# ScalarE's order within an attention step: the copy of a turned block before the next item's exponential

## The chip, the core and the metric

The kernel runs on one core of one Trainium2 chip. The metric is the device time of one execution in microseconds (us), lower is better. Where several runs are given, their median counts. The core's engines each work off a queue of their own in order: TensorE (PE: matrix products and turns, that is transposes), VectorE (DVE), ScalarE (ACT), GpSimd (POOL) and SyncE (SP, which here issues DMAs). They wait for each other on semaphores.

## The reference

Two transformer blocks over 512 tokens of width 1024, in float32. The first has two kinds of attention heads and a convolved, gated feed-forward network (FFN), the second a compressed, a selected/windowed and a sliding-window attention between two FFNs. The edit touches only how the attention phases run. Their mathematics, cut to what matters:

```python
# first block: 4 heads "diff" (two softmax maps, one minus lam times the other)
logits = einsum('bhmqd,bhmkd->bhmqk', q, k) * scale + bias      # masked to k <= q
p = softmax(logits, axis=-1)
out = (p[:, :, 0] - lam * p[:, :, 1]) @ v
# first block: 8 heads "stick breaking"
z = (q @ k.T) * scale
between = cumsum(log_sigmoid(-z), reverse=True) - log_sigmoid(-z)   # over k < q
out = where(strict, exp(log_sigmoid(z) + between), 0) @ v
# second block: 8 heads with keys of the whole past, in two branches, gated and added
out = g[1] * softmax(s_selected) @ v_s + g[2] * softmax(s_window) @ v_w + g[0] * o_compressed
# second block: 8 heads with a window of 128 keys and a sink logit
p = softmax(concat([s, sink]))[..., :-1];  out = p @ v
```

With 512 tokens the selected branch and the wide window both see the whole causal past, so the kernel computes both as dense causal softmax.

## The kernel before

Each product of activations with weights is made as three products of split numbers (a high and a low part of weights and activations), with 128 rows of the contraction and 512 tokens at a time. The weights come in units of 512 KB through a ring of six buffers: SP loads one, ScalarE makes its high part (L531), GpSimd its low part (L543), TensorE uses both.

**The attention phases.** There are two, each run by the same four functions, `pe_attn`, `act_attn`, `dve_attn` and `pool_attn`. The work is a list of *items*. An item is a block of 128 queries of one head (of both maps of one diff head) with its keys, 128 to 512 wide. The first phase has 48 items (kinds `sb`, stick breaking, and `diff`), the second 96 (kind `soft`; the last 32, numbers 64 to 95, have the window of at most 256 keys and a sink). An item m goes through these stations:

1. TensorE, the scores (L930), into PSUM; those of two items m and m+1 (m even) together, for diff items each alone.
2. VectorE prepares the logits in SBUF and their smallest negated value, which is the shift (L1043), or the scan of the stick breaking (L1035 to L1040, after three instructions of ScalarE, L973 to L977).
3. ScalarE, the exponential into the tile `W` (named `sq` in the profile): L984 for sb, L988 twice for diff, L994 for soft, behind one of a single column for the sink, L993. The sum of the row comes with it.
4. VectorE, the reciprocal of the sum (L1067), the gate (L1070) or the sink (L1066), or for diff the combination of both maps (L1056 to L1062).
5. TensorE, the *turn*: up to four transposes of 128x128 (L945) into one of two PSUM banks.
6. ScalarE, the *copy* of the turned block to the tile `WT` (named `tmp` in the profile), L1001.
7. TensorE, the product with V (L954), always into the same PSUM bank.
8. VectorE moves the output out of that bank (L1014, L1017 or L1019).

Every engine runs through steps n. TensorE in step n makes the scores of n and n+1 (n even), then a first part of the fill, the turn of n-2, a second part of the fill, and the product with V of n-3. It waits before the turn for the exponential (diff: the combination) of n-2, and before the product for the copy of n-3 and for the move of output n-4. VectorE in step n moves output n-4, prepares n, and does station 4 for n-1, for which it waits for the exponential of n-1. ScalarE in step n makes its three instructions for an sb item n, the exponential of n-1 and the copy of n-2. Behind that come the *hooks* of the step: a weight unit's high part (L531), the split of queries or keys (L822), the compressed branch's pieces.

**The fill** is what hides all this from TensorE: products of later projections with their weights (L1133, L1122, and L1173 to L1177 for the compressed branch's small network), dealt out by two tables with a number of products for each step. The tables `FILL1` and `FILL2` hold 6 to 8 products a step in most of the first phase and 4 (later 3 to 8) in the second, a pair meaning those before and behind the turn:

```python
FILL2 = [4] * 48 + [6] * 4 + [0] + [6] * 4 + [0] + [3] * 8 + [0] + [3] * 8 + [0] + [3] * 8
FILL2 = FILL2 + [(0, 4), 0] + [(0, 4), (3, 0)] * 5 + [(3, 12), (12, 6), 6]
```

The 16 names of the second fill are used up in order, so a 4 can stand for wide products (512 columns) or for narrow ones (256).

Of the kernel before, what the change touches and what calls it, by code (L numbers as in the profile page):

```python
# [36 lines left out]
ACT = mybir.ActivationFunctionType  # L37
# [164 lines left out]
def build(nc, weights, x_t, params, rows, table_t, bias_line, out_t):  # L202
    with ExitStack() as top:
# [77 lines left out]
        W, WT = sq, tmp  # L281
# [12 lines left out]
        def LM(m, n):  # L294
            return (L0, L1)[m][:, n % 2, :]
# [21 lines left out]
        PS = top.enter_context(nc.psum_tensor("PS", [P, 8, T], F32))  # L317
# [487 lines left out]
        T_PS, PV_PS = 3, 5  # L805
# [154 lines left out]
        def act_attn(act, a, link, after):  # L960
            items = a.items
            for n in range(len(items) + 2):
                for what in a.hooks["act0"].get(n, []):
                    what(act)
                if n < len(items) and items[n].kind == "sb":
                    it = items[n]
                    if n >= 2 and items[n - 2].kind == "diff":
                        act.wait_ge(a.comb, n - 1)
                    elif n >= 2:
                        act.wait_ge(a.s_read, items[n - 2].map0 + 1)  # L970
                    act.wait_ge(a.qk_done, n + 1)
                    z = LM(0, n)[:, 0:it.nk]
                    c = link(act.activation(z, PS[:, it.bank[0], 0:it.nk], ACT.Abs))  # L973
                    after(c)
                    c = link(act.activation(z, z, ACT.Exp, scale=-1.0))
                    after(c)
                    act.activation(z, z, ACT.Ln, bias=1.0).then_inc(a.pre_done, 1)  # L977
                if 1 <= n < len(items) + 1:
                    it = items[n - 1]
                    if it.kind != "diff" and it.n >= 2:  # L980
                        act.wait_ge(a.turned, it.n - 1)
                    act.wait_ge(a.s_read, it.map0 + len(it.maps))
                    if it.kind == "sb":
                        act.activation(W[:, it.n % 2, 0:it.nk], LM(1, it.n)[:, 0:it.nk], ACT.Exp).then_inc(a.exp_done, 1)  # L984
                    elif it.kind == "diff":
                        for m in range(2):
                            z = LM(m, it.n)[:, 0:it.nk]
                            x = act.activation(z, z, ACT.Exp, bias=it.st[:, 2 + m:3 + m], scale=-1.0,  # L988
                                               accum_out=it.st[:, 4 + m:5 + m])
                        x.then_inc(a.exp_done, 1)  # L990
                    else:
                        if it.sink is not None:
                            act.activation(it.st[:, 5:6], it.sink, ACT.Exp, bias=it.st[:, 2:3], scale=-1.0)  # L993
                        act.activation(W[:, it.n % 2, 0:it.nk], LM(0, it.n)[:, 0:it.nk], ACT.Exp,  # L994
                                       bias=it.st[:, 2:3], scale=-1.0, accum_out=it.st[:, 4:5]).then_inc(a.exp_done, 1)
                if n >= 2:
                    it = items[n - 2]
                    act.wait_ge(a.turned, it.n + 1)
                    if it.n >= 2:
                        act.wait_ge(a.pv_done, it.n - 1)  # L1000
                    act.activation(WT[:, it.n % 2, 0:it.nk], PS[:, T_PS + it.n % 2, 0:it.nk], ACT.Copy).then_inc(a.wt_ready, 1)  # L1001
                for what in a.hooks["act"].get(n, []):
                    what(act)

# [665 lines left out]
        def _(act):  # L1670
# [56 lines left out]
            act_next(act, U_DV + 3)  # L1727
            act.preload_act_table_set("natural_log_exp_and_others")
            act_attn(act, at1, link, after)
            act_head(7)(act)  # L1730
            act_turn1(act, 0, 6)
# [50 lines left out]
            act.wait_ge(v_ready[1], TB)  # L1782
            act.activation(gates[:, :, :], V[:, 0, :, 3 * P:NAT2], ACT.Exp, scale=-1.0).then_inc(gate_e, 1)
            act_attn(act, at2, link, after)
            act_turn1(act, 1, 6)
            act_next(act, U_WO2)
# [272 lines left out]
```

## Time and profile before

| | us |
|---|---|
| median of 3 runs | 1677.44 |
| lowest and highest | 1674.91, 1680.5 |
| the profiled execution | 1680.9 |
| its span, first to last instruction | 1678.9 |
| first attention phase in the trace | about 76 to 250 |
| second attention phase | about 1058 to 1274 |

In that execution TensorE is busy for 98% of the span, VectorE and ScalarE for 42% each, GpSimd for 46%. The times in the trace are from the span's start. A row of a timeline has start, duration, engine, line, operation, and what it writes and reads; in brackets, how long the engine had been idle and what ended that. Instructions of TensorE overlap, and so, by some hundredths, do those of ScalarE.

### The profile page before, as it was taken

Reading aid. Unit: us, or ns where it says so; the run is one execution under the profiler, and the core shown is the slowest. Engines: PE = TensorE matmul, PEld = TensorE weight load, DVE = VectorE, ACT = ScalarE, POOL = GpSimd, SP = SyncE. Lnnn points to the kernel's source line nnn. Section 1 sums busy time; section 2 is a strip of 40 time slices with the busy share of each in tenths; the row PEclk is TensorE's granted clock in tenths of the full one; section 3 lists DMA queues with packets and bytes.
Section 4 is the critical chain, followed back from the end, with each engine's and each line's share of the span. In section 5 each row is a group of like instructions: output and inputs, shape, how many; then the busy total and the mean of one; then the engine's idle time right before and its main releaser. Section 6 shows DMA issues by size and latency. Waiting matters only on the chain.

```text
span 1678.9 us, 21453 instructions
## 1 busy us (share of the span) xinstructions
PE 1645.6 (98%) x8168; PEld 1357.1 (81%) x8168; DVE 706.5 (42%) x1402; ACT 697.7 (42%) x1231; POOL 780.4 (46%) x594
## 2 busy tenths in 40 slices
PE   9999989999999999999999999999999999999997
PEld 7777778888888887888888888888778888888885
DVE  6266654884444226312212225655673311112224
ACT  6367755543334224422223225566573422223322
POOL 7434525474445552744444553644112554444550
PEclk9999989999999999999999999999999999999999
DMA  5411102322322331322322322222002322332231
GB/s 200 145 51 51 39 14 100 101 89 100 101 94 94 101 100 51 120 94 100 100 90 99 101 94 94 89 71 70 26 27 76 100 91 98 101 98 91 100 101 50
DMA packets 42117, 147.37 MB, mean 88 GB/s; under 512 B 4768, under 2 KB 5152, under 8 KB 42016
## 3 DMA queue, kind: packets, MB, share of 16 engines
q1 hardware_dynamic: 40536, 143.13, 25.9%
q10 hardware_dynamic: 1480, 2.89, 0.5%
q8 instruction: 65, 1.06, 0.3%
q14 instruction: 36, 0.29, 0.1%
HBM read 142.84 MB, written 3.41 MB: 87 GB/s over the span
## 4 chain that ended last, share of the span: by engine, by line
PE 88%; DVE 5%; ACT 2%; issue 2%; POOL 1%; DMA 1%; DVEq 0%; ACTq 0%; POOLq 0%
PE PS L499 20%; PE PS L501 20%; PE PS L500 20%; PE PS L1133 5%; PE PS L1122 4%; PE PS L954 4%; PE PS L930 3%; PE PS L474 3%; PE PS L945 2%; PE PS L481 1%; PE PS L521 1%; POOL w_lo L543 1%; PE PS L523 1%; PE PS L522 1%; DMA stage<-in_weights 1%
## 5 line engine op out<-in xcount | busy, mean ns | idle before, releaser
L543 POOL TENSOR_TENSOR w_lo<-stage,w_hi 128x512 fp32r<-128x512 f32 x524 | 710.9, 1382 | 703.5 <-ACT w_hi L531 702.9
L531 ACT ACTIVATE w_hi<-stage 128x1024 fp32r<-128x1024 f32 x262 | 274.6, 1056 | 514.0 <-DMA stage<-in_weights 513.8
L499 PE MATMUL PS<-H_hi,w_hi 128*128 128x512 f32 x992 | 387.7, 391 | 0.4 <-DVE rcol L1311 0.4
L501 PE MATMUL PS<-H_hi,w_lo 128*128 128x512 f32 x992 | 386.0, 389 | 0.0
L500 PE MATMUL PS<-H_lo,w_hi 128*128 128x512 f32 x992 | 386.0, 389 | 0.0
L499 PEld LDWEIGHTS PS<-H_hi,w_hi 128*128 128x128 f32 x992 | 186.2, 188 | 39.7 <-issue 1.0
L500 PEld LDWEIGHTS PS<-H_lo,w_hi 128*128 128x128 f32 x992 | 186.2, 188 | 39.6 <-issue 1.0
L501 PEld LDWEIGHTS PS<-H_hi,w_lo 128*128 128x128 f32 x992 | 186.2, 188 | 39.0
L499 PE MATMUL PS<-A_hi,w_hi 128*128 128x512 f32 x528 | 205.7, 390 | 0.4 <-DVE A_lo L653 0.4
L501 PE MATMUL PS<-A_hi,w_lo 128*128 128x512 f32 x528 | 205.5, 389 | 0.0
L500 PE MATMUL PS<-A_lo,w_hi 128*128 128x512 f32 x528 | 205.4, 389 | 0.0
L668 DVE TENSOR_TENSOR conv<-PS,rstd 128x512 f32<-128x512 f32 x88 | 56.5, 685 | 353.2 <-PE PS L501 337.1
L653 DVE TENSOR_TENSOR A_lo<-A,A_hi 128x512 fp32r<-128x512 f32 x66 | 84.0, 1279 | 227.2 <-ACT A_hi L597 227.2
L499 PEld LDWEIGHTS PS<-A_hi,w_hi 128*128 128x128 f32 x528 | 99.1, 188 | 21.8 <-DVE A_lo L653 1.3
L500 PEld LDWEIGHTS PS<-A_lo,w_hi 128*128 128x128 f32 x528 | 99.1, 188 | 20.7
L501 PEld LDWEIGHTS PS<-A_hi,w_lo 128*128 128x128 f32 x528 | 99.1, 188 | 20.4
L954 PEld LDWEIGHTS PS<-V,tmp 128*128 128x128 f32 x672 | 94.9, 195 | 22.1 <-issue 10.1
L954 PE MATMUL PS<-V,tmp 128*128 128x64 f32 (+1 forms) x672 | 95.4, 271 | 8.2 <-DVE O L1017 3.1
L1001 ACT ACTIVATE tmp<-PS 128x256 f32<-128x256 f32 (+3 forms) x144 | 59.4, 413 | 91.9 <-PE PS L945 91.0
L678 DVE SCALAR_TENSOR_TENSOR conv<-tmp,par,conv 128x511 f32<-128x511 f32 (+1 forms) x88 | 77.4, 934 | 6.2 <-ACT conv L620 5.8
L1133 PE MATMUL PS<-H_hi,w_hi 128*128 128x512 f32 x168 | 74.7, 445 | 0.0
L1133 PE MATMUL PS<-H_hi,w_lo 128*128 128x512 f32 x168 | 71.5, 426 | 0.0
(241 smaller groups left out, 2187.8 us busy)
## 6 DMA issues: line engine op xcount, KB each, us to landing
stage<-in_weights SPq DMA_DIRECT2D x262, 512.0 KB, 3.3
out_t<-Y SPq DMA_DIRECT2D x8, 256.0 KB, 2.0
X<-in_x_t SPq DMA_DIRECT2D x3, 512.0 KB, 8.2
bias_line<-bias_line ACTq DMA_DIRECT2D x1, 1270.0 KB
strip<-bias_line ACTq DMA_DIRECT2D x1, 1024.0 KB, 5.0
stage<-in_weights SPq DMA_DIRECT2D x2, 256.0 KB, 4.4
X<-in_x_t ACTq DMA_DIRECT2D x2, 256.0 KB, 5.8
V<-QF SPq DMA_DIRECT2D x4, 128.0 KB, 2.6
```

Source lines behind the costliest of these rows:

```text
L499: pe.matmul(out, a, h_hi, start=first, stop=False, skip_group_check=skip)
L500: pe.matmul(out, a, h_lo, start=False, stop=False, skip_group_check=skip)
L501: return pe.matmul(out, b, h_hi, start=False, stop=last, skip_group_check=skip)
L531: act.activation(w_hi[:, slot, :], stage[:, slot, :], ACT.Copy).then_inc(hi_done, 1)
L543: lo = pool.tensor_tensor(w_lo[:, slot, cols], stage[:, slot, cols], w_hi[:, slot, cols].bitcast(F32), ALU.subtract)
L653: dve.tensor_tensor(A_lo[:, f % DEEP, :], A[:, f, :], A_hi[:, f % DEEP, :].bitcast(F32), ALU.subtract).then_inc(a_lo_done, 1)
L668: dve.tensor_tensor(z[j], PS[:, pair_bank(n) + j, :], rstd[:, :], ALU.mult).then_inc(zs, 1)
L678: dve.scalar_tensor_tensor(out=y, in0=z[j][:, 0:T - back], scalar=c, in1=y, op0=ALU.mult, op1=ALU.add).then_inc(conv_step, 1)
L954: mm = pe.matmul(PS[:, PV_PS, 0:it.dv], WT[:, it.n % 2, bass.ts(kb, P)], it.v[kb], start=(kb == 0), stop=(kb == it.nk // P - 1))
L1001: act.activation(WT[:, it.n % 2, 0:it.nk], PS[:, T_PS + it.n % 2, 0:it.nk], ACT.Copy).then_inc(a.wt_ready, 1)
L1122: mm = pe.matmul(PS[:, j, :], w[:, u % RING, cols], h, start=(g == 0 and x == 0), stop=(g == 7 and x == 2))
L1133: mm = pe.matmul(PS[:, bank, :], w[:, u % RING, bass.ts(k, P)], h[:, k, :], start=(k == 0 and x == 0), stop=(k == KC - 1 and x == 2))
```

## The change

In `act_attn` the piece with the copy (station 6, for item n-2) moves up, ahead of the piece with the exponential (station 3, for item n-1). The three sb instructions of item n stay first and the hooks last. Nothing else is changed. Line numbers move by it: the copy is L983 in the changed kernel, the exponentials are L990 (sb), L994 (diff), L999 (sink) and L1000 (soft).

```diff
                     act.activation(z, z, ACT.Ln, bias=1.0).then_inc(a.pre_done, 1)
+                if n >= 2:
+                    it = items[n - 2]
+                    act.wait_ge(a.turned, it.n + 1)
+                    if it.n >= 2:
+                        act.wait_ge(a.pv_done, it.n - 1)
+                    act.activation(WT[:, it.n % 2, 0:it.nk], PS[:, T_PS + it.n % 2, 0:it.nk], ACT.Copy).then_inc(a.wt_ready, 1)
                 if 1 <= n < len(items) + 1:
                     it = items[n - 1]
...
                         act.activation(W[:, it.n % 2, 0:it.nk], LM(0, it.n)[:, 0:it.nk], ACT.Exp,
                                        bias=it.st[:, 2:3], scale=-1.0, accum_out=it.st[:, 4:5]).then_inc(a.exp_done, 1)
-                if n >= 2:
-                    it = items[n - 2]
-                    act.wait_ge(a.turned, it.n + 1)
-                    if it.n >= 2:
-                        act.wait_ge(a.pv_done, it.n - 1)
-                    act.activation(WT[:, it.n % 2, 0:it.nk], PS[:, T_PS + it.n % 2, 0:it.nk], ACT.Copy).then_inc(a.wt_ready, 1)
```

ScalarE's queue in the second phase, from the exponential of item 39 to the copy of item 40, before. `tmp<-PS` is the copy, `sq,stat<-L,stat` the exponential, and the brackets name the semaphores waited for (`turned`: the turn is done; `s_read`: VectorE has prepared the item):

```order
L994 ACTIVATE sq,stat<-L,stat 128x256 [waits at2_s_read,at2_turned]
L1001 ACTIVATE tmp<-PS 128x256 [waits at2_pv_done,at2_turned]
L531 ACTIVATE w_hi<-stage 128x1024 [waits loaded5]
L994 ACTIVATE sq,stat<-L,stat 128x384 [waits at2_s_read,at2_turned]
L1001 ACTIVATE tmp<-PS 128x256 [waits at2_pv_done,at2_turned]
L994 ACTIVATE sq,stat<-L,stat 128x384 [waits at2_s_read,at2_turned]
L1001 ACTIVATE tmp<-PS 128x384 [waits at2_pv_done,at2_turned]
```

The same place after:

```order
L983 ACTIVATE tmp<-PS 128x256 [waits at2_pv_done,at2_turned]
L1000 ACTIVATE sq,stat<-L,stat 128x256 [waits at2_s_read,at2_turned]
L531 ACTIVATE w_hi<-stage 128x1024 [waits loaded5]
L983 ACTIVATE tmp<-PS 128x256 [waits at2_pv_done,at2_turned]
L1000 ACTIVATE sq,stat<-L,stat 128x384 [waits at2_s_read,at2_turned]
L983 ACTIVATE tmp<-PS 128x384 [waits at2_pv_done,at2_turned]
L1000 ACTIVATE sq,stat<-L,stat 128x384 [waits at2_s_read,at2_turned]
```

Each copy has moved ahead of the exponential that stood before it; the hook (`w_hi<-stage`) keeps its place. The first phase, where the fourth diff item of the first group (512 keys) meets the next group's first sb item, before:

```order
L977 ACTIVATE L<-L 128x128 [waits act_self]
L988 ACTIVATE L,stat<-L,stat 128x512 [waits at1_s_read]
L988 ACTIVATE L,stat<-L,stat 128x512
L1001 ACTIVATE tmp<-PS 128x384 [waits at1_pv_done,at1_turned]
L973 ACTIVATE L<-PS 128x128 [waits at1_qk_done,at1_comb]
```

And after:

```order
L977 ACTIVATE L<-L 128x128 [waits act_self]
L983 ACTIVATE tmp<-PS 128x384 [waits at1_pv_done,at1_turned]
L994 ACTIVATE L,stat<-L,stat 128x512 [waits at1_s_read]
L994 ACTIVATE L,stat<-L,stat 128x512
L973 ACTIVATE L<-PS 128x128 [waits at1_qk_done,at1_comb]
```

Here both exponentials of the diff item now stand behind the copy, and so behind the turn that it waits for. The instructions of TensorE, VectorE, GpSimd and SP keep their order.

## Rows read from the trace of the kernel before

**Rows 1.** The page, busy us, share of the span and instructions

```profile
PE 1645.6 (98%) x8168; PEld 1357.1 (81%) x8168; DVE 706.5 (42%) x1402; ACT 697.7 (42%) x1231; POOL 780.4 (46%) x594
```

**Rows 2.** Busy time by stretch (stretch, its us; each engine's busy us; granted clock, DMA)

```profile
76.00:240.00 164.00, 154.85 (x962) 124.32 (x961) 113.94 (x283) 114.85 (x283) 69.09 (x57) 0.97 0.13 43
1058.00:1274.00 216.00, 209.04 (x1527) 174.78 (x1526) 125.16 (x533) 131.71 (x377) 68.25 (x51) 0.98 0.16 50
```

**Rows 3.** Waits of TensorE and its weight loads: total us, times, longest

```profile
PE PS L954 <- ACT tmp L1001: 1.0, 3, 0.5
...
PEld PS L954 <- ACT tmp L1001: 4.9, 6, 1.5
```

**Rows 4.** Waits of ScalarE

```profile
ACT tmp L1001 <- PE PS L945: 91.0, 74, 5.9
...
ACT L L973 <- PE PS L936: 15.8, 15, 1.7
```

**Rows 5.** Timeline, items 24 and 25: turns, copy 24, exponential 25, product 24

```profile
1109.10 0.49 PE L945 MATMUL PS<-ident,sq 128*128 128x128 f32 x3
...
1109.62 0.49 ACT L1001 ACTIVATE tmp<-PS 128x384 f32<-128x384 f32 x1 [0.33 <-PE PS L945]
...
1110.01 0.61 ACT L994 ACTIVATE sq<-L,stat 128x384 f32<-128x384 f32 x1
...
1110.29 0.49 PE L945 MATMUL PS<-ident,sq 128*128 128x128 f32 x3
1110.52 0.19 ACT L994 ACTIVATION_READ_ACCUMULATOR sq<-L,stat 128x1 f32 x1
...
1110.85 0.78 PE L954 MATMUL PS<-V,tmp 128*128 128x64 f32 x6
```

**Rows 6.** Timeline: end of exponential 37, copy 36, VectorE's move 35, product 36

```profile
1135.26 0.19 ACT L994 ACTIVATION_READ_ACCUMULATOR sq<-L,stat 128x1 f32 x1
...
1135.35 0.37 ACT L1001 ACTIVATE tmp<-PS 128x256 f32<-128x256 f32 x1
...
1136.11 0.28 DVE L1014 SCALAR_TENSOR_TENSOR O<-PS,stat,O 128x64 f32<-128x64 f32 x1 [0.21 <-DVE stat L1070]
...
1136.54 0.52 PE L954 MATMUL PS<-V,tmp 128*128 128x64 f32 x3 [0.25 <-ACT tmp L1001]
```

**Rows 7.** Timeline, items 68 and 69 of the window part

```profile
1218.95 0.38 PE L945 MATMUL PS<-ident,sq 128*128 128x128 f32 x2
...
1219.37 0.38 ACT L1001 ACTIVATE tmp<-PS 128x256 f32<-128x256 f32 x1 [1.73 <-PE PS L945]
...
1219.65 0.28 ACT L993 ACTIVATE stat<-row,stat 128x1 f32<-128x1 f32 x1
...
1220.23 0.19 ACT L994 ACTIVATION_READ_ACCUMULATOR sq<-L,stat 128x1 f32 x1
1220.31 0.38 PE L945 MATMUL PS<-ident,sq 128*128 128x128 f32 x2
...
1220.76 0.55 PE L954 MATMUL PS<-V,tmp 128*128 128x64 f32 x4
```

**Rows 8.** Timeline, diff items 10 and 11 of the first phase

```profile
115.96 0.49 PE L945 MATMUL PS<-ident,sq 128*128 128x128 f32 x3
116.00 0.71 ACT L988 ACTIVATE L<-L,stat 128x512 f32<-128x512 f32 x1
...
117.32 0.19 ACT L988 ACTIVATION_READ_ACCUMULATOR L<-L,stat 128x1 f32 x1
...
117.41 0.47 ACT L1001 ACTIVATE tmp<-PS 128x384 f32<-128x384 f32 x1
...
118.86 0.66 PE L945 MATMUL PS<-ident,sq 128*128 128x128 f32 x4 [0.34 <-DVE sq L1062]
```

**Rows 9.** Busy time by stretch, TensorE's granted clock in the third column from the right

```profile
1192.00:1200.00 8.00, 5.25 (x36) 4.12 (x36) 6.74 (x24) 3.78 (x8) 0.00 (x0) 1.00 0.01 2
1200.00:1208.00 8.00, 8.00 (x40) 6.86 (x41) 3.32 (x15) 2.46 (x7) 0.00 (x0) 0.57 0.00 1
```

## The prediction, made before the changed kernel had run

> **What bounds the kernel now.** I read the page's busy times first, then the busy times by stretch, the waits of TensorE and of ScalarE, and last the timeline of single steps. TensorE is busy for 98% of the span [rows 1], and it stays at 94% and 97% in the two attention phases, the only places that the edit touches [rows 2]. So a ScalarE instruction costs or gives time only where TensorE stands still for it. The weight products that fill the attention steps are the cover: TensorE has other work while a block goes through ScalarE and VectorE. The cover differs from step to step. The score products of two items are issued together, in the even steps; in an odd step of the second phase there lie only the fill, one turn and one product with V between two turns. I call those the short steps. ScalarE is not short of time: it waits 91.0 us in 74 places for a turn to end before it copies the block [rows 4].
>
> **What the change does to the order.** Let m be an item. Before, ScalarE makes exp(m) as soon as VectorE has prepared it, and then waits for turn(m-1) to copy that block. So exp(m) is usually finished while TensorE is still on its way to turn(m-1). After, ScalarE waits for turn(m-1), copies, and only then makes exp(m). No instruction is added or taken; 142 pairs change places, DMAs and the queues of SP and GpSimd keep theirs. The wait that becomes new is exp(m) behind turn(m-1), and behind exp(m) stand turn(m) on TensorE and, on VectorE, the sum's reciprocal, the gate and the move of output m-2 out of the one PV bank, for which product m-1 waits.
>
> **First term, the leg to the next turn.** An item of the second phase, 384 keys wide: turn(24) ends at 1109.10 + 0.49 = 1109.59, the copy takes 0.49 and starts 0.03 later, exp(25) with its sum takes from 1110.01 to 1110.52 + 0.19, that is 0.70 [rows 5]. ACT's instructions overlap by 0.06. In the new order exp(25) ends at 1109.62 + 0.49 - 0.06 + 0.70 = 1110.75 and turn(25) can start 0.05 later, at 1110.80. It started at 1110.29 [rows 5]: 0.5 us late. In the window part an item has a sink exponential too: turn(68) ends 1219.33, copy 0.38, exponentials 1219.65 to 1220.42 (0.77), new end 1220.46, turn(69) 0.2 us late [rows 7]. In the even steps the score products lie between, and the same sum leaves 0.5 to 2 us of margin.
>
> **Second term, the leg through VectorE.** The trace of before shows this leg where exp was not ahead: exp(37) ends 1135.26 + 0.19 = 1135.45, reciprocal and the gate's multiply follow, the output is moved from 1136.11 to 1136.39, and product 36 starts at 1136.54 [rows 6]. That is 1.09 us from the end of the exponential to the product with V; with the small differences between items I take 1.0. In the new order that ends at 1110.75 + 1.0 = 1111.75 for product 24, which started at 1110.85 [rows 5]: 0.9 late. For product 68 it is 1220.46 + 1.0 = 1221.46 against 1220.76 [rows 7]: 0.7. The later of the two legs is the stall of the step, the first one is contained in it. The same rows say what the wait list's ScalarE entries are worth: the trace puts 0.25 us of product 36 on the copy [rows 6], but the copy of that item ended at 1135.35 + 0.37 = 1135.72 [rows 6], and the product came 0.15 us after VectorE's move. So the 1.0 us in 3 places that TensorE seems to wait for copies (4.9 us on its weight loads) [rows 3] are this leg already, and I count no gain from the earlier copy.
>
> **The sum.** I worked both legs for each item, carrying the delay along (turns, products, moves and hooks later by all stalls so far). Second phase: items 1 to 16 stall 6 times, 1.1 us together (the fill there is four 512-column products, the cover just holds); items 17 to 48, 14 times, 8.6 us (no or narrower fill beside the short steps; [rows 5] is one of them); items 49 to 64, 4 times, 1.5 us; items 65 to 80, 8 times, 5.7 us ([rows 7] is one); items 81 to 95, 13 times, 4.7 us. That is 21.6 us. Between 1184 and 1200 us VectorE also has the compressed branch's work between the reciprocal and the move; where exp comes late there it holds that up too, by under 1 us at two steps, which I leave to the range. First phase: a stick-breaking item's exponential is one instruction of 0.3 to 0.6 us and in the even steps ScalarE waits for the score products anyway (15.8 us in 15 places) [rows 4], so I count 0.1. A diff item's is two of 0.71 with their sums, 116.00 to 117.51, and VectorE needs 1.35 us to combine them before the turn at 118.86. New: turn(10) ends 116.45, copy 0.47, exponentials end 118.40, turn(11) can start 1.35 later at 119.75, 0.9 late [rows 8]. Per group of four diff items that gives 1.05, 1.05, 1.3 and, in the last group whose short step has no fill, 1.7: with the 0.1 it is 5.2. All of it lies on the path, because TensorE has nothing else in its queue order. **Sum: 21.6 + 5.2 = 26.8 us.** The profiled execution took 1680.9 us (span 1678.9), 3.5 over the median of the three runs; on its own base that is 1707.7, on the median 1677.4 + 26.8 = 1704.2. I take **1704**.
>
> **Rivals.** *Only the first leg.* If VectorE's moves have slack that I miss, the stalls are those of the turns: 8.6 in the second phase and 5.2 in the first, 13.8 us, 1691. Against it is that [rows 6] shows the leg acting; for it that I add delays item by item, which may count one twice.
> *The clock.* Behind a stretch in which TensorE was busy for 5.25 of 8 us its mean granted clock over the next 8 us was 0.57 [rows 9]: the lower of its two levels (1.2 GHz) for most of them, which cost 8 x 0.43 = 3.4 us. Stalls of 0.7 to 0.9 us in every 3.5 us would leave TensorE busy for some 78%, between that stretch (66%) and the mean of the phase (97% at a mean clock of 0.98) [rows 2]. One to four more such stretches cost 3 to 13 us: 1707 to 1717, taken as 1713. The Trainium skill (TensorE: Matmul & The Clock Gate, "A second HAM failure mode: psum-queue depth-cycling") says that frequent short idles between groups of matmuls can make the clock go back and forth. By that rule the dips would come all along both phases, against which only the rows of before speak, where short idles kept the clock.
> *Faster: copies free TensorE.* If the waits listed on the copy are real, the earlier copy removes them, 1.0 + 4.9 us [rows 3], and 1677.4 - 5.9 = 1671.5. It decides this way if the copy, not the move, releases the product with V, and if the exponentials' delay of 1 to 3 us stays within the cover, that is if TensorE's distance from one turn's end to the next turn's start is over 1.2 us (copy, exponential and two hand-overs). In [rows 5] it is 0.70. The Trainium skill (PSUM — Partial Sum Buffer, "Summary: rules for kernel authors") advises to evacuate promptly, which is what the edit does; by that rule it would come out on this side.
> *No change.* The delays fall into idle time that is there already (TensorE is idle for 7.0 us in the second phase [rows 2]); 1677 to 1682. Against it: that idle lies at other steps.
> That the edit doesn't take effect is excluded by the instruction order, which shows the exchange at every step.
>
> **How the numbers follow.** Both legs as worked, 1695 to 1713: 0.62, likeliest. First leg only: 0.12. Clock on top: 0.13. No change: 0.06. Faster: 0.07. A measurement of this kernel can tell about 0.3%, 5 us. So faster 0.07, same 0.06, slower 0.87. The range holds the first, most of the clock's and of the one-leg case: **1687 to 1717**.
>
> **What would show it.** In the profile after: ScalarE's wait for the turns stays near 90 us, but exp starts behind the copy everywhere. In TensorE's waits, the turn of the sq block behind ScalarE's exponential and the product with V behind VectorE's move of O grow from a few us to 15 or 20 together; L945 waits for VectorE's combine in all four diff groups by some 0.9 us more. The phase 1058 to 1274 becomes 21 to 25 us longer, 76 to 240 about 5, the FFN stages equal. Wrong if the turns keep their distance of 0.7 us in the short steps, or if the granted clock falls in stretches that had it full.

## The result and the profile after

The changed kernel takes **1716.0 us** (median of 5 runs, 1714.0 to 1717.67), the kernel before 1680.5 in the same comparison (5 runs, 1674.91 to 1682.48): ratio 1.0214, 95% interval 1.0201 to 1.0228, slower by 2.1%. The profiled execution took 1714.0 us with a span of 1711.9, 33.0 over the span of before. The forecast was 1704, range 1687 to 1717: right in its sign and its range, 26.8 us where 33.0 (profiles) or 35.5 (medians) came.

The lengths of the two attention phases come from the first and the last turn in each. First the kernel before, TensorE's timeline, the turns of items 0 and 47 of the first phase and 0 and 95 of the second (start, us):

```profile
82.77 0.27 PE L945 MATMUL PS<-ident,sq 128*128 128x128 f32 x1
...
245.09 0.27 PE L945 MATMUL PS<-ident,sq 128*128 128x128 f32 x1
...
1062.13 0.28 PE L945 MATMUL PS<-ident,sq 128*128 128x128 f32 x1
...
1269.75 0.28 PE L945 MATMUL PS<-ident,sq 128*128 128x128 f32 x1
```

The same four turns after:

```profile
83.17 0.27 PE L945 MATMUL PS<-ident,sq 128*128 128x128 f32 x1
...
250.32 0.27 PE L945 MATMUL PS<-ident,sq 128*128 128x128 f32 x1
...
1067.23 0.27 PE L945 MATMUL PS<-ident,sq 128*128 128x128 f32 x1
...
1302.95 0.27 PE L945 MATMUL PS<-ident,sq 128*128 128x128 f32 x1
```

The first phase is 167.15 us long where it was 162.32 (+4.83), the second 235.72 where it was 207.62 (+28.10). Together that is 32.9 of the 33.0 us; of the rest no part differs by more than 0.4 us. Laid side by side turn by turn, the second phase grows like this (forecast, then measured): items 1 to 16 1.1 and 1.2; 17 to 48 8.6 and 12.7; 49 to 64 1.5 and 1.6; 65 to 80 5.7 and 9.2; 81 to 95 4.7 and 3.4.

TensorE's waits after (total us, times, longest), to be read against [rows 3]:

```profile
PE PS L954 <- DVE O L1017: 10.4, 18, 1.7
PE PS L945 <- DVE sq L1062: 6.7, 5, 1.9
PE PS L954 <- DVE O L1014: 5.0, 9, 2.1
PE PS L945 <- ACT sq L1000: 4.4, 9, 1.2
...
PE PS L954 <- ACT tmp L983: 2.0, 5, 0.6
PE PS L954 <- DVE O L1019: 1.7, 5, 0.6
```

The same rows of the kernel before:

```profile
PE PS L954 <- DVE O L1017: 3.1, 6, 1.3
...
PE PS L954 <- DVE O L1019: 2.3, 6, 0.6
...
PE PS L945 <- DVE sq L1062: 1.9, 4, 0.8
...
PE PS L954 <- DVE O L1014: 1.5, 1, 1.5
```

The product with V (L954) now waits 15.4 us for VectorE's moves of the softmax outputs (L1014 and L1017) where it waited 4.6: the second leg of the prediction. L945 behind the exponential (4.4 us, 0.7 before) is the first. The copy was put ahead so that the product finds its block sooner, and yet its wait for the copy grew too, from 1.0 [rows 3] to 2.0. The weight loads (PEld), which overlap with the products, so that not all of this is lost, wait 16.9 us for the copy instead of 4.9 [rows 3], and 12.9 us for the exponential where it was 1.3:

```profile
PEld PS L954 <- ACT tmp L983: 16.9, 22, 1.4
...
PEld PS L945 <- ACT sq L1000: 12.9, 29, 1.7
```

ScalarE's wait for the turns grew as well:

```profile
ACT tmp L983 <- PE PS L945: 143.9, 100, 6.1
```

It was 91.0 us in 74 places [rows 4]. ScalarE now stands in front of the turn with nothing done, and makes the exponential afterwards.

The short step of [rows 5] after the change, TensorE, ScalarE and VectorE on the timeline, turn 24 to product 24:

```profile
1118.03 0.49 PE L945 MATMUL PS<-ident,sq 128*128 128x128 f32 x3
...
1118.55 0.49 ACT L983 ACTIVATE tmp<-PS 128x384 f32<-128x384 f32 x1 [0.86 <-PE PS L945]
...
1118.94 0.61 ACT L1000 ACTIVATE sq<-L,stat 128x384 f32<-128x384 f32 x1
...
1119.45 0.19 ACT L1000 ACTIVATION_READ_ACCUMULATOR sq<-L,stat 128x1 f32 x1
1119.67 0.16 DVE L1067 RECIPROCAL stat<-stat 128x1 f32<-128x1 f32 x1 [1.24 <-ACT sq L1000]
...
1119.69 0.55 PE L945 MATMUL PS<-ident,sq 128*128 128x128 f32 x3 [0.31 <-ACT sq L1000]
...
1120.30 0.28 DVE L1014 SCALAR_TENSOR_TENSOR O<-PS,stat,O 128x64 f32<-128x64 f32 x1 [0.21 <-DVE stat L1070]
...
1120.73 0.52 PE L954 MATMUL PS<-V,tmp 128*128 128x64 f32 x3 [0.26 <-DVE O L1014]
```

The step reads as it was worked out. The exponential ends at 1119.45 + 0.19 = 1119.64, turn 25 starts 0.05 later, and product 24 1.09 after the exponential's end (1.0 had been taken). From turn 24 to turn 25 it is 1.66 us, where it was 1.19 [rows 5]: 0.47 of the 0.51 that the leg gives. The other 0.04 is a misreading in the forecast: in [rows 5] two instructions of ScalarE overlap by 0.10 (the copy ends at 1109.62 + 0.49 = 1110.11, the exponential starts at 1110.01), where 0.06 had been taken. From turn 24 to product 24 it is 2.70 where it was 1.75: 0.95, against 0.9.

### The profile page after: what moved, and what is told of

It is laid out like the page before. It is cut to its first block, busy times and chain, and to the rows that moved or that the text cites. A ratio compares the mean times of both kernels' runs of the same rounds, so it can differ in the third digit from the quotient of the medians.

```text
span 1711.9 us, 21453 instructions
## 1 busy us (share of the span) xinstructions
PE 1657.6 (97%) x8168; PEld 1356.0 (79%) x8168; DVE 704.6 (41%) x1402; ACT 697.0 (41%) x1231; POOL 782.3 (46%) x594
## 4 chain that ended last, share of the span: by engine, by line
PE 87%; DVE 5%; ACT 4%; issue 3%; DMA 1%; POOL 1%; DVEq 0%; ACTq 0%; POOLq 0%
PE PS L499 20%; PE PS L500 20%; PE PS L501 20%; PE PS L1122 5%; PE PS L1133 5%; PE PS L954 3%; PE PS L930 3%; PE PS L474 3%; PE PS L945 2%; PE PS L481 1%; PE PS L521 1%; PE PS L523 1%; PE PS L522 1%; ACT sq L1000 1%; DVE H_lo L454 1%
## 5 line engine op out<-in xcount | busy, mean ns | idle before, releaser
L501 PE MATMUL PS<-H_hi,w_lo 128*128 128x512 f32 x992 | 385.9, 389 | 0.0
L954 PEld LDWEIGHTS PS<-V,tmp 128*128 128x128 f32 x672 | 93.4, 194 | 39.3 <-ACT tmp L983 16.9
L983 ACT ACTIVATE tmp<-PS 128x256 f32<-128x256 f32 (+3 forms) x144 | 59.9, 416 | 144.1 <-PE PS L945 143.9
L954 PE MATMUL PS<-V,tmp 128*128 128x64 f32 (+1 forms) x672 | 96.8, 273 | 19.6 <-DVE O L1017 10.4
L945 PE MATMUL PS<-ident,sq 128*128 128x128 f32 x336 | 63.8, 284 | 12.0 <-DVE sq L1062 6.7
```

The source lines that it names most:

```text
L501: return pe.matmul(out, b, h_hi, start=False, stop=last, skip_group_check=skip)
L945: mm = pe.transpose(PS[:, T_PS + it.n % 2, bass.ts(kb, P)], W[:, it.n % 2, bass.ts(kb, P)], ident[:, :])
L954: mm = pe.matmul(PS[:, PV_PS, 0:it.dv], WT[:, it.n % 2, bass.ts(kb, P)], it.v[kb], start=(kb == 0), stop=(kb == it.nk // P - 1))
```

## The experiments

Each kernel was timed beside the kernel before on the same chip; three chips served, on which the median of before was 1677.83 (first four kernels), 1681.26 (next three and the second look at the kernel before) and 1678.8 (the last two). "Phase 2" below is the distance from the first to the last turn there, 207.62 us before.

**One phase at a time.**

```diff
+                if n >= 2 and a is at1:      # in the second kernel: a is at2
+                    ... the copy of item n - 2 ...
                 if 1 <= n < len(items) + 1:
                     ... the exponential of item n - 1 ...
-                if n >= 2:
+                if n >= 2 and not (a is at1):
```

> Copy ahead of the exponential in the first phase only. The traces of before and after, laid side by side turn by turn, give the first phase +4.8 us, all of it at the second diff item of each group and the two behind it. Theory (the cost is exp behind turn, copy): +4 to +6 us over the kernel before, ratio 1.002 to 1.004, the second phase as before (216 us from its start to its end). Rival (what the first phase does shifts the second, so the parts don't add): over +8 or under +2.

Measured: 1683.3 us, ratio 1.0045 (1.0026 to 1.0064), +5.5 by the medians. The first phase is 4.66 us longer in the trace, in the same places as after: +1.07 at turn 11, +1.08 at 23, +1.31 at 34 and 35, +1.49 at 46. Its second phase is not as before but 3.15 us shorter: the stretch of half clock of [rows 9] (TensorE's granted clock at the lower of its two levels, 1.2 GHz) is missing (more on this below, at the second look at the kernel before).

> Copy first in the second phase only. Theory: +26 to +31 us (the traces give +28.1 between the phase's first and last turn), ratio 1.016 to 1.018; with the first phase alone it adds up to the whole change's 33 to 35. Rival: the cost of the two phases doesn't add, under +24.

Measured: 1708.89 us, ratio 1.0186 (1.017 to 1.0201), +31.1, at the upper end of the expectation; phase 2 grows by 27.5. The two phases add up: 4.7 + 27.5 = 32.2 in the traces against 32.9 for the whole change, 36.5 against 35.5 in the medians.

**Even or odd exponentials.** The swap in the second phase, made only at the steps whose exponential belongs to an even item (n odd) or an odd one (n even):

```diff
+                if n >= 2 and a is at2 and n % 2 == 1:      # in the second kernel: n % 2 == 0
+                    ... the copy of item n - 2 ...
...
-                if n >= 2:
+                if n >= 2 and not (a is at2 and n % 2 == 1):
```

> Copy first only where the exponential is that of an even item of the second phase (the next turn's step then holds the score products of two items). Theory (margin of 0.5 to 2 us there): 0 for all steps but one; at item 32 the copy stands behind ScalarE's hook that waits for GpSimd, so exp 32 comes late there: 1.0 us, up to 4.5 if TensorE's clock falls behind it as it did after the whole change. So 0 to +5 us. Rival (the earlier copy frees TensorE, the exponential has cover): -1 to -6 us.

Measured: 1686.3 us, ratio 1.0054 (1.0039 to 1.0069), +8.5, more than the upper end of the expectation; phase 2 +5.15. The place foreseen is there; ScalarE and TensorE at item 32:

```profile
1127.88 1.03 ACT L1351 ACTIVATE kp_hi<-scratch 128x992 fp32r<-128x992 f32 x1 [3.61 <-POOL scratch L1345]
...
1128.81 0.58 ACT L983 ACTIVATE tmp<-PS 128x512 f32<-128x512 f32 x1
...
1129.29 0.39 ACT L1000 ACTIVATE sq<-L,stat 128x128 f32<-128x128 f32 x1
...
1129.83 0.33 PE L945 MATMUL PS<-ident,sq 128*128 128x128 f32 x1 [1.38 <-ACT sq L1000]
```

ScalarE waits 3.61 us for GpSimd's windows (a hook), then copies item 31 (0.58 us, the widest block), and only then makes exponential 32, for which TensorE stands still 1.38 us: +1.18 at this turn. Not foreseen were +0.3 at turn 20, +0.6 at turn 36, +1.45 at turn 51 (in a stretch of half clock) and +0.3 to +0.8 at each of several turns between 83 and 91 (the window part, where an even step's score products are short too), in part by a second stretch of half clock. Each lasted 3.4 us; the kernel before had one of 6.8.

> Copy first only where the exponential is that of an odd item of the second phase (the next turn lies in a short step, without score products). Theory: nearly the whole of the second phase's cost, +22 to +28 us. Rival (every step pays, since copy and exponential of each item now stand in one chain): about half, +12 to +16.

Measured: 1707.05 us, ratio 1.0177 (1.0162 to 1.0192), +29.2, just above the expectation; phase 2 +25.55, of the 27.5 that the swap at all steps cost in its trace. Even + odd is 30.7 us against 27.5. The surplus lies at items 81 to 95, where the even swaps alone cost 3.9 us (with a stretch of half clock, at most 1.7 of it), the odd ones alone 3.4 and all together 3.4. The rival, that every step pays alike, is out. The cost lies in the short steps. In this trace items 17 to 48 grow by 8.7 us, where the two legs had given 8.6.

**The leg through VectorE.** In the second phase the output of item n-3 is moved out of the PV bank ahead of the reciprocal of item n-1, in the same step of VectorE, instead of at the start of the next one (phase 1 keeps its order):

```diff
-                if n >= 4:
-                    ... move of items[n - 4] ...
+                if a is not at2 and n >= 4:
+                    move(items[n - 4])
                 ... preparation of item n ...
+                if a is at2 and 3 <= n < len(items) + 3:
+                    move(items[n - 3])
                 ... reciprocal, gate of item n - 1 ...
```

> The changed kernel, and in the second phase VectorE moves output m-2 out of the PV bank ahead of the reciprocal of item m, not behind it. So product m-1 no longer waits for exponential m through VectorE. Theory of two legs (the later leg through VectorE sets each short step's stall): only the first leg is left. 8.6 us in the second phase, 2 to 4 us at items 32 to 34, 5 in the first phase and 0 to 3 of clock: +14 to +20 us over the kernel before, 1691 to 1698, that is 14 to 20 us faster than the changed kernel; the waits of the product with V for VectorE's O fall from 15.4 us under 5. Rival (the turn's leg alone sets the stalls, or the clock does): within 5 us of the changed kernel, 1709 to 1714.

> The kernel before with the same early move of the output in the second phase, ScalarE's order unchanged. Before, the product with V waits 4.6 us in the second phase for VectorE's move, most of it at items 57 to 60, where VectorE has the compressed branch's work between reciprocal and move, and the stretch of half clock behind it costs 3.4 us. Theory: -2 to -7 us. Rival (VectorE waits for the product and so delays reciprocals and preparations of later items): 0 to +4 us.

Measured, on the changed kernel: 1692.71 us, ratio 1.0061 (1.0039 to 1.0083), +11.5; on the kernel before: 1676.23 us, ratio 0.9974 (0.9962 to 0.9986), -5.0. The rival for the changed kernel, that it would stay within 5 us of its time, is far out: moving an output of 64 columns earlier takes back two thirds of the loss. Its waits after, on TensorE:

```profile
PE PS L945 <- DVE sq L1068: 6.7, 5, 1.9
PE PS L945 <- ACT sq L1000: 5.2, 12, 1.4
...
PE PS L954 <- DVE O L1019: 1.7, 5, 0.6
...
PE PS L954 <- ACT tmp L983: 0.6, 1, 0.6
...
PE PS L954 <- DVE O L1017: 0.4, 2, 0.2
...
PE PS L954 <- DVE O L1014: 0.3, 1, 0.3
```

The product's wait for the softmax outputs fell from 15.4 us to 0.7 and the turn's wait for the exponential stayed: one leg is gone and the other is there. The place of [rows 5] in this kernel:

```profile
1118.31 0.49 PE L945 MATMUL PS<-ident,sq 128*128 128x128 f32 x3
...
1119.46 0.28 DVE L1014 SCALAR_TENSOR_TENSOR O<-PS,stat,O 128x64 f32<-128x64 f32 x1 [0.52 <-PE PS L954]
1119.73 0.19 ACT L1000 ACTIVATION_READ_ACCUMULATOR sq<-L,stat 128x1 f32 x1
...
1119.97 0.55 PE L945 MATMUL PS<-ident,sq 128*128 128x128 f32 x3 [0.32 <-ACT sq L1000]
...
1120.59 0.78 PE L954 MATMUL PS<-V,tmp 128*128 128x64 f32 x6
```

Turn 25 is as late as after the change (1.66 us behind turn 24), product 24 follows it without a wait. The gain was larger than expected (11.5 over before, where 14 to 20 was written), because the expectation counted the move as a repair only. The kernel before gains by it too. Against the second look at the kernel before, its phase 2 is 6.49 us shorter: 1.6 are gained up to item 48 and 6.8 between 49 and 64 (3.15 of them is the stretch of half clock that is missing here too), and 1.8 are given back between 65 and 74. Comparing the two kernels that have the early move isolates the first leg: 3.94 + 6.36 (6.49 less the 0.13 by which the two looks at before differ) = 10.3 us, at most 1.7 of it a stretch of half clock (3.4 us long) that only the one has. That leaves 8.6 or somewhat more, and of these 1.2 are the stall behind GpSimd at item 32; so the first leg itself is 7.4 or somewhat more, where 8.6 was forecast for it alone.

**The windows' copy one step later.** ScalarE's hook that waits for GpSimd, and GpSimd's that follows it, on the changed kernel:

```diff
-            hook(at2, "act", at + 1, act_windows(s))
-            hook(at2, "pool", at + 2, pool_windows_lo(s))
+            hook(at2, "act", at + 2, act_windows(s))
+            hook(at2, "pool", at + 3, pool_windows_lo(s))
```

> The changed kernel with ScalarE's copy of the compression windows (which waits for GpSimd) and GpSimd's subtraction behind it hooked one step later. In the changed kernel copy 31 and exponential 32 stand behind that wait and turns 32 to 34 come 3.6 us late in all, 2.1 more than the two legs give; the clock was at half speed behind them (3.4 us). Theory: 3 to 6 us faster than the changed kernel, +29 to +32 over the kernel before; turn 32 has no wait for the exponential over 0.3 us. Rival (those steps stall anyway by the two legs): within 1.5 us of the changed kernel.

Measured: 1711.09 us, ratio 1.0184 (1.0167 to 1.0202), +29.8, within the expectation (5.0 less than the whole change by the two ratios, whose intervals just touch). In the trace turns 32 to 34 come 4.52 us earlier relative to the phase's start. Busy time by stretch shows both parts of it, first in the changed kernel (stretch and its us; busy us of PE, PEld, DVE, ACT, POOL; granted clock; DMA):

```profile
1138.00:1140.00 2.00, 0.77 (x4) 0.34 (x4) 0.16 (x1) 1.80 (x4) 0.98 (x1) 1.00 0.00 0
1140.00:1148.00 8.00, 7.76 (x37) 6.46 (x36) 3.47 (x17) 2.11 (x10) 1.30 (x1) 0.57 0.19 66
```

and in this one, in the same stretches:

```profile
1138.00:1140.00 2.00, 2.00 (x20) 1.78 (x19) 0.95 (x6) 1.17 (x4) 1.61 (x1) 1.00 0.00 0
1140.00:1148.00 8.00, 7.48 (x60) 6.15 (x58) 4.90 (x23) 5.06 (x17) 4.48 (x3) 1.00 0.21 69
```

Turn 32 stood for 1.23 us in the changed kernel, TensorE was busy for 0.77 of 2 us, and behind that the mean granted clock was 0.57 for 8 us: mostly the lower of the two levels, 1.2 GHz, 8 x 0.43 = 3.4 us at most. With the hook later neither is there. But this trace has other such stretches at 1184 to 1188 and 1212 to 1232 us (3.4 and 10.2 us long), and its own span is no shorter: the phase's total moved by -1.2 only. The profiled execution was the slowest of the four (1714.59 us; the others 1710.22 to 1711.34), so the trace shows where the time went, and the saving itself rests on the ratios alone. Taking away one stretch of half clock did not take away the tendency to have some.

**The additions out of the leg.** The four additions of the compressed branch (VectorE, 0.69 us each) go from the end of their step to its start, on the changed kernel:

```diff
-            hook(at2, "dve", at + 19 + 2 * pair, dve_cmp_add(pair))
+            hook(at2, "dve0", at + 19 + 2 * pair, dve_cmp_add(pair))
```

> The changed kernel with VectorE's four additions of the compressed branch's product (0.69 us each) ahead of the preparation in their step and no longer between reciprocal and move. In the changed kernel turns 66 to 72 each come 1.2 us late for every short step, where the two legs give 0.7. Theory: these steps fall back to 0.7, 1.5 to 2.5 us faster than the changed kernel, +31 to +33 over the kernel before; the wait of product 67 to 71 for VectorE's O falls from 0.9 to 0.4. Rival (the addition has cover, the extra comes from the clock or the fill): the 0.9 stays, within 0.5 us of the changed kernel.

Measured: 1713.33 us, ratio 1.02 (1.0184 to 1.0216): +34.5, against +35.5. That misses the +31 to +33 expected, and the two intervals overlap. But what was named in the trace is there. In the changed kernel, VectorE and TensorE at product 68:

```profile
1243.36 0.16 DVE L1067 RECIPROCAL stat<-stat 128x1 f32<-128x1 f32 x1
...
1243.67 0.69 DVE L1524 TENSOR_TENSOR O<-PS,O 128x512 f32<-128x512 f32 x1
...
1244.28 0.28 DVE L1017 TENSOR_SCALAR O<-PS,stat 128x64 f32<-128x64 f32 x1
...
1244.70 0.52 PE L954 MATMUL PS<-V,tmp 128*128 128x64 f32 x3 [0.89 <-DVE O L1017]
```

and with the addition moved:

```profile
1244.82 0.16 DVE L1067 RECIPROCAL stat<-stat 128x1 f32<-128x1 f32 x1
...
1245.13 0.28 DVE L1017 TENSOR_SCALAR O<-PS,stat 128x64 f32<-128x64 f32 x1
...
1245.56 0.63 PE L954 MATMUL PS<-V,tmp 128*128 128x64 f32 x4 [0.30 <-ACT tmp L983]
```

The wait falls from 0.89 to 0.30, and the turns 68, 70, 72 and 74 come 0.58, 0.60, 0.59 and, with a stretch of half clock gone beside it, 1.05 us earlier. That is 2.4 us for the additions, as expected. But between turns 48 and 64, which the edit doesn't touch, this trace is 2.6 us longer than that of the changed kernel, with more half clock (10.2 us long between 1212 and 1232 us, against 3.4). The times alone couldn't tell the two theories apart; the trace did.

**The kernel before a second time.**

> The kernel before, unchanged, for a second profile: which of its stretches at half clock come back at the same place. The turns should lie within 0.1 us of the first profile's outside those stretches. If the stretch at 1200 to 1208 us (3.4 us) comes from the idle time ahead of it alone, it is there again; if it depends on something that the program doesn't set, it may be gone.

Measured: 1682.54 us. Outside the half-clock stretches the turns of phase 2 agree within 0.2 us with the first profile's. The stretch of [rows 9] is there again, 2 us later as all of phase 2 is (columns as above):

```profile
1194.00:1202.00 8.00, 5.23 (x36) 4.14 (x36) 6.74 (x24) 3.77 (x8) 0.00 (x0) 1.00 0.01 2
...
1202.00:1210.00 8.00, 8.00 (x40) 6.87 (x41) 3.37 (x15) 2.47 (x7) 0.00 (x0) 0.57 0.00 1
```

But the kernel with the swap in the first phase only, whose second phase is instruction for instruction that of before and started 4.8 us later than in the first profile, has it not. The same two stretches, 4.8 us later:

```profile
1196.80:1204.80 8.00, 5.22 (x36) 4.13 (x36) 6.74 (x24) 3.75 (x8) 0.00 (x0) 1.00 0.01 2
1204.80:1212.80 8.00, 8.00 (x69) 7.10 (x70) 4.87 (x20) 4.01 (x13) 0.00 (x0) 1.00 0.20 65
```

TensorE was busy for 5.22 of 8 us ahead of them, as in the other two, and the clock stayed full; the phase is 3.15 us shorter for it. So the idle time ahead doesn't decide alone. Outside phase 2 the two looks at before differ as well: the second had 13.7 us of half clock between 213 and 231 us where the first had 10.2, and its first phase is 1.51 us longer.

**A version that beats both.** The kernel before with the early move and the additions first:

> The kernel before with the early move in the second phase (5.0 us faster in its run, by the medians) and the additions of the compressed branch ahead of the preparation. With the early move alone turns 68 to 74 came 0.45 us late each, since TensorE's next compressed product waited for the addition. Theory: 1.5 to 2 us more, so -5 to -8 us against the kernel before, ratio 0.995 to 0.997. Rival (the next preparation is delayed by the addition, 0.7 us in a step without margin): as with the move alone or 1 to 3 us slower, ratio 0.997 to 0.999.

Measured: 1674.38 us, ratio 0.9964 (0.995 to 0.9977), 4.4 us (0.36%) faster than the kernel before and 2.4% faster than the changed one. In its trace turns 68 to 74 come 0.45, 0.44, 0.45 and 0.49 us earlier than with the move alone, 1.8 together, as expected; and phase 2 is 199.36 us long, 8.3 shorter than before, 3.15 of it the stretch of half clock behind the compressed branch's work. The intervals of this kernel and of the early move alone overlap, so that the additions gain something here is shown by the trace only. By the medians it is 0.6 us short of the lower saving expected (5).

## Why the prediction was right, and where it was short

**The mechanism holds at every step looked at.** Both legs act, with the numbers of [rows 5] to [rows 8]: 0.47 for 0.51 on the turn, 0.95 for 0.9 on the product. The first leg alone is 7.4 us or somewhat more in the second phase by the two kernels with the early move, 8.6 by the forecast's sum. The rival *only the first leg* (1691) is out: the product's wait for the moves rose by 10.8 us and the early move took it away.

**First phase: 5.2 forecast, 4.8 measured**, but as a sum of errors on both sides. The diff groups gave 1.09, 1.08, 1.32 and 1.49 (forecast 1.05, 1.05, 1.3, 1.7), 4.98 together. Turn 47 came another 1.60 late, with a stretch of half clock of 3.4 us between turns 46 and 47 that before had not. It belongs to the edit: all five kernels with the swap in the first phase have one, starting between 242.9 and 246.9 us, and none of the seven others has; the forecast had no term for it. Against this, 1.98 us were gained between turns 35 and 43, where the clock was at half for 3.4 us and in the first profile of before for 10.2. That was luck and not the swap: the changed kernel with the early move and the second look at before both had 13.7 us of it there, and between turns 38 and 43 they differ by 0.2 us. Their first phases are 170.27 and 163.83 us long, so in this pair, with the same luck on both sides, the first phase costs 6.4.

**Items 17 to 48: 8.6 forecast, 12.7 measured.** The step that failed is "the same sum leaves 0.5 to 2 us of margin" in the even steps. It failed above all at item 32, where the copy that went ahead stands behind ScalarE's hook that waits for GpSimd, and is the widest of its group. I had moved the hooks along with the stalls, but hadn't asked what the copy, itself behind a hook, would do to the exponential that now followed it. With the odd swaps only, this group grows by 8.7; the 3.9 us above that are the stall at turn 32 (1.0) and the half clock behind it (2.9).

**Items 65 to 80: 5.7 forecast, 9.2 measured.** Mis-sized was the second leg's 1.0 us: it was read where nothing lay between reciprocal and move [rows 6]. Here VectorE's addition of 0.69 us lies between, four times: 2.4 us by its experiment. A stretch of half clock is 0.7 (the kernel with the swap in the second phase only, which has none there, grows by 8.5). For items 57 to 60, where the reductions of the compressed branch lie there, the prediction named this and left it to the range. Those steps lost up to 1.3 us each. That the term for 49 to 64 came out right (1.6 for 1.5) is luck: these items had 3.4 us of half clock after and 6.8 before. Against the kernel with the swap in the first phase only, whose second phase is that of before with none, they grow by 4.7, of which the half clock can be 1.7 at most.

**Items 81 to 95: 4.7 forecast, 3.4 measured.** The worry noted at the one-leg rival, that delays added item by item may count one twice, may have been right here, by 1.3 us. The surplus of the even and odd halves lies at the same items, but no run isolates the cause.

**The clock.** It was a rival of its own (1713, 0.13) and is partly true: in phase 2 three stretches of half clock (6.8, 3.4 and 3.4 us long) where before had one of 6.8, in the first phase two of 3.4 where before had 10.2 us. Half of all time at half clock is 14.1 us after and 12.0 before, but this is only the most that it can cost: a stretch of 3.4 us cost 1.6 us at turn 47 and 0.7 between items 65 and 80, where TensorE waits part of the time anyway.

Of the 6.1 us by which the two phases passed the forecast, items 17 to 48 make 4.1 (item 32 with the half clock behind it), items 65 to 80 3.5 (additions 2.4, half clock 0.7, the rest open), items 1 to 16 and 49 to 64 0.1 each, items 81 to 95 -1.3 and the first phase -0.4 (1.6 more behind turn 46, 2.0 less by the luck of the clock).

The Trainium skill (TensorE: Matmul & The Clock Gate, "A second HAM failure mode: psum-queue depth-cycling") describes a clock that swings where TensorE idles briefly between groups of matmuls. The traces agree only in part: in phase 2 of the changed kernel 35 waits of at most 0.9 us and six longer ones left the clock at its full level nearly all the time, at a mean of 0.97.

**The faster rival** (1671.5) is out by 44.5 us: the waits listed on the copy grew instead of going. The Trainium skill's advice to evacuate promptly (PSUM — Partial Sum Buffer, "Summary: rules for kernel authors") did not help here. The reason that the Trainium skill gives there is that the space is tight, and neither trace has a turn that waited for its bank; what waited was the exponential behind the copy.

**The signs in the profile.** ScalarE's wait for the turns was to stay near 90 us and rose to 143.9: in the kernel before, the exponential was made inside this waiting time. That number should have been the first to move. The second phase was to become 21 to 25 us longer and became 28.1 longer. The waits on VectorE's O and on the exponential were to grow "to 15 or 20 together"; they are 19.8 (15.4 + 4.4), and L945's wait for the combine rose from 1.9 to 6.7, both as told. The turns' distance of 0.7 us grew to 1.17 in the step of [rows 5]. But the other sign of being wrong did come: the granted clock fell in stretches that had it full, behind turn 32, behind product 72 and behind turn 46 of the first phase. The forecast's 26.8 us are the two legs alone and have no term for this; only the upper part of its range had.

## What to carry to other kernels

In this kernel, where the queues are worked off in order and TensorE sets the time, an instruction of ScalarE whose input is ready belongs ahead of one that waits for TensorE. Put the waiting one first and all behind it is made after the hand-over instead of during it; what that costs is the turn-around (here copy, exponential, reciprocal, move) less the work that TensorE has between two hand-overs, so look at the steps with the least of it, and at every helper instruction that lies in the chain there. The same reading finds gains: the move of a finished output stood behind a reciprocal it didn't need, and bringing it forward made the kernel before 0.3% faster.

## What the runs showed of the hardware that was not expected

- The stretches of half clock (3.4 to 10.2 us long) are not set by the program alone: the same instructions had one of 6.8 us in two executions and none in a third that reached the place 4.8 us later, with the same idle time ahead. The time goes with them: of nine executions of the kernel before on one chip, the three with a mean granted clock of 0.991 had spans of 1680.4 to 1680.6 us, the three at 0.993 1678.5 to 1679.6 and the three at 0.995 or 0.996 1676.0 to 1676.6.
- Short idle times in many steps do not bring the clock down each time. The three stretches in phase 2 of the changed kernel and the one of before each had a wait of TensorE of over a microsecond shortly ahead (1.23 us at turn 32, 1.74 at product 58, 1.24 at product 72; before 1.50 at product 60). Not each such wait had one behind it: the longest of the changed kernel's phase 2, 2.08 us at 1221, had none. And one stretch of the kernel with the even swaps, at 1170 us, came behind two waits of only 0.66 and 0.64 us.
- A wait that is put down to one releaser may have a second one just behind it: product 68 with the addition moved waits 0.30 us for the copy, which ends at 1245.45, but VectorE's move ends at 1245.13 + 0.28 = 1245.41. An earlier copy alone would have gained 0.04 us there.
